# Rotary embedding in a two-block kernel: the halves of the heads swapped by transfers in place of fp32 matmuls

## The reference, cut to what matters

```python
x1, x2 = xf[..., :half], xf[..., half:]
return jnp.concatenate([x1 * cos - x2 * sin, x1 * sin + x2 * cos], axis=-1)
```

## Time and profile before

| | us |
|---|---|
| median of 3 runs | 2641.88 (2640.23 to 2644.57) |
| profiled execution, its own time | 2636.38 |
| its span in the trace | 2634.6 |
| PE busy | 2469.4 |
| DVE, ACT, POOL busy | 1277.0, 972.6, 1253.4 |

### The profile page before, as it was taken

The page is one execution under the profiler, slowest core; times in us unless marked ns, Lnnn a source line. Parts: engine busy times, 40 slices in busy tenths (PEclk is TensorE's granted clock), DMA queues, the critical chain, the costliest instruction groups (busy, mean ns, idle before and its releaser), DMA issues. The chain is left out here.

```text
span 2634.6 us, 33864 instructions
## 1 busy us (share of the span) xinstructions
PE 2469.4 (94%) x12515; PEld 1968.4 (75%) x12515; DVE 1277.0 (48%) x2482; ACT 972.6 (37%) x1560; POOL 1253.4 (48%) x1638
## 2 busy tenths in 40 slices
PE   5899889999999999989999999998896999999998
PEld 4678568888888778856788878887563667788887
DVE  6884553353335668454333234246688753612211
ACT  5233333332222433334333232244335874523322
POOL 5443334556556634433465545555332433455553
PEclk9999999999999999989999999999987999999999
DMA  4232222333222332222233222233210001233222
GB/s 143 73 89 69 65 66 82 104 105 104 96 96 90 95 97 73 77 60 69 77 104 120 96 96 91 94 99 109 88 51 8 1 17 57 80 97 98 94 96 88
DMA packets 80291, 218.62 MB, mean 83 GB/s; under 512 B 15744, under 2 KB 25344, under 8 KB 79616
## 3 DMA queue, kind: packets, MB, share of 16 engines
q1 hardware_dynamic: 60912, 200.96, 23.7%
q10 hardware_dynamic: 19216, 15.51, 2.1%
HBM read 207.78 MB, written 2.10 MB: 80 GB/s over the span
## 5 line engine op out<-in xcount | busy, mean ns | idle before, releaser
L870 POOL TENSOR_TENSOR w_lo<-w_raw,w_hi 128x256 fp32r<-128x256 f32 x1494 | 1170.6, 814 | 1237.3 <-ACT w_hi L1405 1237.3
L930 PE MATMUL psG<-h_hi,w_hi 128*128 128x512 f32 x1880 | 756.0, 402 | 25.5 <-POOL w_lo L870 21.3
L931 PE MATMUL psG<-h_lo,w_hi 128*128 128x512 f32 x1880 | 739.7, 393 | 0.0
L932 PE MATMUL psG<-h_hi,w_lo 128*128 128x512 f32 x1880 | 738.9, 393 | 0.0
L1405 ACT ACTIVATE w_hi<-w_raw 128x1024 fp32r<-128x1024 f32 (+4 forms) x417 | 403.9, 969 | 511.3 <-PE psG L932 497.3
L930 PEld LDWEIGHTS psG<-h_hi,w_hi 128*128 128x128 f32 x1880 | 358.4, 191 | 115.8 <-issue 34.2
L932 PEld LDWEIGHTS psG<-h_hi,w_lo 128*128 128x128 f32 x1880 | 357.4, 190 | 76.8
L931 PEld LDWEIGHTS psG<-h_lo,w_hi 128*128 128x128 f32 x1880 | 358.8, 191 | 75.0 <-issue 2.9
L930 PE MATMUL psG<-m_hi,w_hi 128*128 128x512 f32 x800 | 311.6, 390 | 1.1 <-DVE m_lo L1857 1.1
L932 PE MATMUL psG<-m_hi,w_lo 128*128 128x512 f32 x800 | 311.3, 389 | 0.0
L931 PE MATMUL psG<-m_lo,w_hi 128*128 128x512 f32 x800 | 311.2, 389 | 0.0
(11 more groups left out here) (327 smaller groups left out, 2783.4 us busy)
## 6 DMA issues: line engine op xcount, KB each, us to landing
w_raw<-wstream SPq DMA_DIRECT2D x327, 512.0 KB, 3.3
w_raw<-wstream SPq DMA_DIRECT2D x64, 256.0 KB, 2.6
w_raw<-wstream SPq DMA_DIRECT2D x16, 384.0 KB, 3.0
work_b<-work_b ACTq DMA_DIRECT2D x16, 256.0 KB, 3.6
work_b<-cmpw ACTq DMA_DIRECT2D x2, 2048.0 KB, 8.0
x<-xT SPq DMA_DIRECT2D x4, 512.0 KB, 6.4
small_work<-ssmp ACTq DMA_DIRECT2D x8, 256.0 KB, 4.0
outT<-x SPq DMA_DIRECT2D x1, 2048.0 KB, 6.3
```

The lines of the kernel that those rows point to most:

```text
L870: ins = pool.tensor_tensor(lo[:, c], w[:, c], hi[:, c].bitcast(F32), ALU.subtract)
L930: pe.matmul(out, whi, hi, start=(k == 0), stop=False)
L931: pe.matmul(out, whi, lo, start=False, stop=False)
L932: ins = pe.matmul(out, wlo, hi, start=False, stop=(k == K - 1))
```

## The change

The matrix `rot1` is gone; `rot2` swaps halves without a sign, and is used only for the kinds "ln" and "cmpk". The sine tables hold the sign: minus in the first half of a head, plus in the second. Where ACT takes a tile that is to be rotated, it now issues four transfers from its own queue (two heads, two halves each) that write the swapped halves from the raw tile straight into the destination: 8 partitions of 2 KB each in the layers, 32 partitions in the second block. It issues them ahead of the rounding of the next weights. DVE waits for them (`s_swap`, `s_swap2`), multiplies the destination by the sine table in place, the raw tile by the cosine table, and adds.

In the layers features 16 to 63 of a head are not swapped, so `qT1` and `kT1` are cleared by POOL: once at the start and once in the second layer, ahead of the low part of the weights of ("u", 1, 3). ACT waits for it (`s_cleared`) ahead of its first transfers of a layer. The jobs ("rot", l, i) use no bank any more; their place in the plan stays, for DVE.

In the second block the kinds "rms", "rope" and "qrms" lose their matmul. "rms" keys are multiplied by their gain as ACT takes them; DVE inverts the root, turns the unscaled key (`turn`) and multiplies by the inverse last, all in the wave of the mean, where the scaled key used to be rotated one wave later.

```diff
-            if what == "job":
+            if what == "job" and key[0] != "rot":
...
-                r[base + d + half, base + d] = -1.0
+                r[base + d + half, base + d] = 1.0
...
-        st[:half], st[half:2 * half] = si, si
+        st[:half], st[half:2 * half] = -si, si
...
-                  "ln": ("", "cmean", "mean", "rot"), "rms": ("", "mean", "rot"), "rope": ("", "rot"), "qrms": ("", "query"), "xqrms": ("", "query")}
+                  "ln": ("", "cmean", "mean", "rot"), "rms": ("", "mean"), "rope": ("", "turn"), "qrms": ("", "query"), "xqrms": ("", "query")}
...
+        swaps = [0] * 4
+        for p in block2_posts:
+            if p["kind"] in ("rms", "rope", "qrms"):
+                swaps[p["i"] % 4] += 4 * 16
+                p["swapped"] = s_swap2[p["i"] % 4], swaps[p["i"] % 4]
+
+        def turned(dst, src, pieces):
+
+            return [(dst[h + to:h + to + n], src[h + at:h + at + n]) for h in (0, HEAD) for to, at, n in pieces]
...
+            def clear_rope_out():
+
+                pool.memset(qT1, 0.0)
+                pool.memset(kT1, 0.0).then_inc(s_cleared, 1)
+
+            clear_rope_out()
             for n in range(len(weights)):
+                if n == tile_of["u", 1, 0] + SPLIT_SLOTS:
+                    pool.wait_ge(s_job, tile_of["u", 1, 0])
+                    clear_rope_out()
...
-                pe.matmul(free_bank(key), rots[1], rawt[:, r % 2, :], start=True, stop=True).then_inc(s_rot, 1)
...
-                    if kind == "qrms":
-                        pe.wait_ge(s_p["raw"], p["raw"])
-                        if p["rotd"] > 1:
-                            pe.wait_ge(s_p["rotd"], p["rotd"] - 1)
-                        pe.matmul(psS[:, 1, 0:N], rots[2], rt, start=True, stop=True).then_inc(s_p["rot"], 1)
...
-                    if p["tile"] is None:
+                    if p["gain"] is None or p["kind"] == "lat":
                         do(act.activation(rt, bank, ACT.Copy), s_p["raw"])
                     else:
 
-                        do(act.activation(rt if p["kind"] == "qrms" else p["dest"], bank, ACT.Copy,
+                        do(act.activation(p["dest"] if p["kind"] == "xqrms" else rt, bank, ACT.Copy,
                                           scale=par(*p["gain"])), s_p["raw"])
...
+                if "swapped" in p:
+                    for dst, src in turned(p["dest"], rt, ((0, 32, 32), (32, 0, 32))):
+                        act.dma_start(dst, src).then_inc(p["swapped"][0], 16)
                 round_after(p["key"])
...
-                    act.sem_inc(s_rawt, 1)
+                    dest = qT1[:, key[2]] if kind == "q" else kT1
+                    if r % 5 == 0:
+                        act.wait_ge(s_cleared, l + 1)
+                    for dst, src in turned(dest, rawt[:, r % 2, :], ((0, 8, 8), (8, 0, 8))):
+                        act.dma_start(dst, src).then_inc(s_swap[r % 2], 16)
...
-                    dve.wait_ge(s_rot, r + 1)
+                    dve.wait_ge(s_swap[r % 2], 4 * 16 * (r // 2 + 1))
                     dest = qT1[:, i] if i < 4 else kT1
-                    tt(tmp[:, 0, :], psG[:, number[key] % GEMM_BANKS, :], tabs[1], ALU.mult, s_took["dve"])
+                    tt(dest, dest, tabs[1], ALU.mult)
                     tt(tmp[:, 1, :], rawt[:, r % 2, :], tabs[0], ALU.mult)
-                    tt(dest, tmp[:, 0, :], tmp[:, 1, :], ALU.add, s_rope)
+                    tt(dest, dest, tmp[:, 1, :], ALU.add, s_rope)
...
+            def turn(p, rt, done=None):
+
+                C, S = tabs
+                dve.wait_ge(s_p["raw"], p["raw"])
+                tt(tmp[:, 2, :], rt, C, ALU.mult)
+                dve.wait_ge(*p["swapped"])
+                tt(p["dest"], p["dest"], S, ALU.mult)
+                tt(p["dest"], p["dest"], tmp[:, 2, :], ALU.add, done)
...
+                    elif kind == "rms":
+                        turn(p, rt)
+                        tt(p["dest"], p["dest"], r, ALU.mult, s_p["out"])
                     else:
                         stt(rt, rt, par(*p["gain"]), r, ALU.mult, ALU.mult, s_p["qn"])
...
                     if kind == "qrms":
-                        dve.wait_ge(s_p["rot"], p["rot"])
-                        tt(tmp[:, 2, :], psS[:, 1, :], S, ALU.mult, s_p["rotd"])
-                        tt(p["dest"], rt, C, ALU.mult)
-                        tt(p["dest"], p["dest"], tmp[:, 2, :], ALU.add, s_p["out"])
+                        turn(p, rt, s_p["out"])
+                elif phase == "turn":
+                    turn(p, rt, s_p["out"])
```

More of the change, by code:

```diff
@@ L138, in job_plan @@
 def job_plan():
-    shape = {"u": (8, "act"), "q": (8, "act"), "k": (8, "act"), "v": (8, "act"), "rot": (0, "dve"), "vt": (0, "act"),
+    shape = {"u": (8, "act"), "q": (8, "act"), "k": (8, "act"), "v": (8, "act"), "vt": (0, "act"),
              "cc": (8, "act"), "cx": (8, "dve"), "cb": (8, "dve"), "glu": (4, "act"), "g0": (8, "act"), "g1": (8, "act"),
@@ L303, in pack_ssm @@
     return out
-CONST_MATS = ("ident", "ones", "blk", "rot1", "rot2")
+CONST_MATS = ("ident", "ones", "blk", "rot2")
 CONST_AT = {n: i * P for i, n in enumerate(CONST_MATS)}
@@ L335, in rotation @@
             for d in range(half):
-                r[base + d + half, base + d] = -1.0
+                r[base + d + half, base + d] = 1.0
                 r[base + d, base + d + half] = 1.0
         return r
-    put("rot1", rotation(8))
     put("rot2", rotation(32))
@@ L501, in block_program @@
         ident, ones, blk = con("ident", P), con("ones", P), con("blk", P)
-        rots = {1: con("rot1", P), 2: con("rot2", P)}
+        halves_swapped = con("rot2", P)
         tabs = con("C1", SEQ), con("S1", SEQ)
@@ L540, in block_program @@
         v = {n: sem("ssm_" + n) for n in names}
-        s_rawt, s_rot, s_rope = sem("rope_in"), sem("rotated"), sem("roped")
+        s_rope, s_cleared = sem("roped"), sem("rope_out_cleared")
+        s_swap = [sem(f"halves_swapped{i}") for i in range(2)]
+        s_swap2 = [sem(f"halves_swapped_block2_{i}") for i in range(4)]
         s_vraw, s_vt, s_vtok = sem("v_raw"), sem("v_transposed"), sem("v_tok")
@@ L807, in block_program @@
                         step(p, "rot", "rotd", "out")
+                    elif phase == "turn":
+                        step(p, "out")
                     elif phase == "query":
-                        step(p, "mean", "sd", *(("rot", "rotd") if p["kind"] == "qrms" else ()), "out")
+                        step(p, "mean", "sd", "out")
                     elif phase == "tok":
@@ L1179, in unit_step @@
                     unit_pv(us[i - 1])
-            def rotate(key):
-                r = key[1] * 5 + key[2]
-                pe.wait_ge(s_rawt, r + 1)
-                pe.matmul(free_bank(key), rots[1], rawt[:, r % 2, :], start=True, stop=True).then_inc(s_rot, 1)
             def values_to_partitions(l):
@@ L1239, in phase_of @@
                     ins.then_inc(s_p["mean"], 1)
-                    if kind == "qrms":
-                        pe.wait_ge(s_p["raw"], p["raw"])
-                        if p["rotd"] > 1:
-                            pe.wait_ge(s_p["rotd"], p["rotd"] - 1)
-                        pe.matmul(psS[:, 1, 0:N], rots[2], rt, start=True, stop=True).then_inc(s_p["rot"], 1)
                 elif phase == "rot":
-                    if "qn" in p:
-                        pe.wait_ge(s_p["qn"], p["qn"])
-                    else:
-                        pe.wait_ge(s_p["raw"], p["raw"])
+                    pe.wait_ge(s_p["qn"], p["qn"])
                     if p["rotd"] > 1:
                         pe.wait_ge(s_p["rotd"], p["rotd"] - 1)
-                    pe.matmul(psS[:, 1, 0:N], rots[2], rt, start=True, stop=True).then_inc(s_p["rot"], 1)
+                    pe.matmul(psS[:, 1, 0:N], halves_swapped, rt, start=True, stop=True).then_inc(s_p["rot"], 1)
                 elif phase == "tok":
@@ L1333, in _ @@
                     elif key[0] == "rot":
-                        rotate(key)
+                        pass
                     elif key[0] == "vt":
```

1 line of the change is left out of this document (removed).

## The result

The changed kernel took 2658.68 us (median of 4 runs, 2656.79 to 2660.42) against 2641.06 (4 runs, 2637.82 to 2644.57): ratio 1.0066, 95% interval 1.0049 to 1.0084. It is slower by 17.6 us. The forecast was +4.3 us, and its range ended at 2655.

What follows compares the result with a forecast made beforehand. PE was busy 94% of the span, but waits for DVE and ACT were taken to decide: first layer +2.5, second layer -0.6, block 2 +2.1, POOL +0.3, sum +4.3 us on 2641.88, so 2646 us; range 2628 to 2655.

Steps and rivals of the forecast that it cites:

- The first layer: First layer up to the scan products: DVE late through k's halves, PE waits 2.5 us more for it, +2.5 us.
- POOL's fills: Clearing with zeros on POOL, at the start and in the second layer: 0.3 us, between 0 and 4.
- the root that releases DVE: Block 2, first sliding key: its root, releasing DVE at 1862.87, is queued behind the next key's issues, +5.6 us.
- the 7.03 us of PE at the second rotation: First layer: PE's wait there for DVE isn't won; PE runs ahead and waits for ACT later.
- The rival of cheap issues: Issues cost 0.34 us or less each on ACT's queue: -5.3 us in all, 2636.6 us; chance 0.22.
- The state matmuls at 936.65 wait for ACT's copy, now behind q0's issues: +2.5: Second layer: PE's state matmuls start 2.5 us later; the layer as a whole comes to -0.6 us.
- the stall of 4.5 us further on: Second layer: PE waits 4.5 us for ACT's copy, ending at 984.4, and its clock falls; 3.4 us lost.
- window matmuls start at 1884.05 as before: Block 2: PE, having lost three stalls and four rotations, waits for DVE; the window matmuls' start does not move.
- the stretch without idle that was to keep 2.1 us whole: Block 2, from 1957.76: DVE runs without idle until attention starts, so +2.1 us stays whole.
- elsewhere PE works without a gap and any shift is carried to the end one for one: Outside block 2's projections and the two layers' rotations: PE has no idle, so shifts reach the end unchanged.
- ACT becomes the pace: Block 2's query waves: issues ahead of roots grow three DVE waits, 7.5 us in place of 2.1; +9.7, 2651.6 us; chance 0.26.
- The slow side: Whole kernel slower by over 0.2%: the ACT case and the upper tail of the forecast, chance 0.30.

Runs made afterwards that it cites:

- experiment 6: Changed kernel plus unused matmuls ahead of two sets of state matmuls (second layer) and both sets of window matmuls (block 2): 2649.72 us, ratio 1.0045 to the kernel before.
- experiment 5: Changed kernel with ACT rounding the next weights before it issues a take's four transfers: 2647.45 us, ratio 1.0033 to the kernel before.
- experiment 2: Changed kernel without any of the 100 transfers, so the swap of halves is left out: 2632.65 us, ratio 0.9980 to the kernel before.
- experiment 8: The kernel before, unchanged, run and traced a second time: 2640.91 us.
- experiment 7: Kernel before with the change in the second layer alone, its transfers issued by SP: 2634.42 us, ratio 0.9981 to the kernel before.

## Why the prediction was wrong

**Right.** The price of an issue (0.62 forecast, 0.61 and 0.63 measured). The first layer: copy, k's halves, DVE's last rotation and the scan products each within 0.5 us. POOL's fills: 2.3 us, and a shift of 0.4 (0.3). The delay of the second layer's state matmuls, 2.7 (2.5), and in block 2 that of the root that releases DVE, 5.9 (5.6). That the 7.03 us of PE at the second rotation would not be won, and that with cheap issues DVE would be the next bound of the second layer: there PE waits for it ahead of the scan products, 0.42 us without transfers and 2.53 with issues by SP.

**Right by luck.** The scan products of the first layer were forecast with PE waiting for DVE at full clock; PE was just as late itself, by a slow clock that the sum didn't have. The rival of cheap issues had been put at -5.3 us, and without any issue the ratio gives 5.3 us; but its stages had been put at -0.6, -4.7 and -0.3, and in the trace they are -2.0, -9.9 and +2.3, with scatter between them.

**The step that failed in the second layer** is "The state matmuls at 936.65 wait for ACT's copy, now behind q0's issues: +2.5". The delay was right, its price wasn't: I priced a fall of the clock behind the stall of 4.5 us further on, and none behind this new one of 3.0. It cost 7.6 and not 2.5 (experiment 6: 2.5 with PE kept busy). The forecast for the layer was -0.6; with the 5.1 added it is +4.5, and 3.8 was measured.

**The step that failed in block 2** is that "window matmuls start at 1884.05 as before", with nothing lost behind them. Its chain up to DVE's release was right. But the forecast had the rotations that PE no longer does, and the turns that DVE does, come out even from there: the window matmuls began 2.0 us later. And they, which had no wait before, got one of 6.86 and ran at half clock: 3.1 us, and 2.2 more to the next product, for which the sum had no term. That makes 7.3 us in place of 0. Of the whole 10.9 us, moving the rounding ahead of the issues gives 6.6 back (experiment 5), and 2.3 stay without any transfer (experiment 2). From there DVE does wait: its row at 1957.76 moved by 1979.10 - 1957.76 - 11.1 = 10.2 us and not by 2.0, so the stretch without idle that was to keep 2.1 us whole carried all of it to attention.

**The frame.** That "elsewhere PE works without a gap and any shift is carried to the end one for one" is wrong as well: PE waits 3.2 and 2.96 us for DVE at 191.68 and 317.36, and the execution of the same kernel whose clock fell behind them was 4.6 us later at attention (experiment 8). It made no difference to the forecast, which stood on the median, but it makes 4.6 of the 22 us between the two first traces.

**The rivals.** "ACT becomes the pace" named the engine and the sign, and its price, +9.7 in all, was too small since it counted the roots and neither weights nor clock. The slow side had 0.30; the range ended 3.7 us under the result because its upper end was that rival and fills of 4 us, with no term for the clock.

**Open.** Why one landing in experiment 7 took 1.5 us longer than its like; how much of the 3.4 to 5.4 us of landings, beside the 2 us of DVE's wait in the second layer, is load on the DMA engines; and why the same wait is followed by half clock in one execution and by full clock in another. No experiment separates these.

## What to carry to other kernels

A transfer that is issued from a compute engine's queue costs that queue the time of the issue, here 0.6 us each within SBUF, for 8 partitions as for 32 (a load from DRAM 0.34); count issues times that price ahead of everything queued behind them, above all work that feeds other engines, and if a queue exists whose next wait ends later anyway, issue there. When a change takes work from the busiest engine and gives it new waits, price each new wait twice: by its length, and by the slower clock of what runs behind it. Do not take the length of a wait for its cost: an engine that has lost work comes early and waits longer. Compare the start of the same instruction instead. Compare stages over more than one execution of the old kernel before giving a step of 1 to 5 us to the change.

## What the runs showed of the hardware

The granted clock was the surprise. The same 128 window matmuls took 3.92 us behind unused matmuls and a wait of 0.18, and 6.07 behind a fill that left 1.75; behind waits of 2.72 and 2.73 they took 7.04 in one kernel and 5.04 in another. And waits of 3.2 and 2.96 us, alike in two executions of one kernel, were followed by full clock in the first and by 0.72 and 0.69 in the second, which lost 2.6 and 2.7 us there. In these rows the length of a wait does not tell how slow the work behind it is. The Trainium skill, page TensorE: Matmul & The Clock Gate, section Part 1: The HAM clock gate (the "warmup" mystery), calls the slow level the default state, which activity releases; the traces agree: in experiment 6 ACT's copy came as late as in after, and the fill alone brought the state matmuls from 0.64 to 0.39 us a pair.

An issue costs SP's queue what it costs ACT's (0.625 and 0.632 us median for the 8-partition transfers), and 32 partitions cost no more than 8 (0.612).
